# A new order from the latent projection to the heads, expert 2's gate and up loaded early, and the last two experts reordered

## The reference

```
layer 0: x += short_conv_mixer(rms_norm(x));  x += hier_moe(rms_norm(x))
layer 1: x += mla_mixer(rms_norm(x));         x += hier_moe(rms_norm(x))

mla_mixer:  lat = h @ w_down                        # 1024 -> 384 (q) + 256 (kv) + 64 (k rope)
            q = rms_norm(lat_q) @ w_q_up            # 8 heads of 128 + 64
            k_nope, v = rms_norm(lat_kv) @ w_kv_up  # 8 heads of 128 + 128
            per head: rms_norm of q and k, rope on the last 64, softmax(q k') v, then @ w_out
hier_moe:   best group of 8, then best 2 of its 8 experts, for each token;
            y = (silu(x @ w_gate[e]) * (x @ w_up[e])) @ w_down[e],  out += gate * y
```

## Time and profile before

| what | value |
|---|---|
| time, median of 3 runs | 2654.95 us (2654.09 to 2657.17) |
| the profiled execution's own time | 2654.59 us |
| its span, first to last instruction | 2652.9 us |
| PE busy in the span | 2321.1 us (87%) |
| DVE, ACT, POOL busy | 810.5, 627.6, 718.7 us |
| mean granted PE clock | 0.943 of full |
| DMA moved | 693 MB, 261 GB/s over the span |

### The profile page before, as it was taken

The page is one execution under the profiler, slowest core; times in us unless marked ns, Lnnn a source line. Parts: engine busy times, 40 slices in busy tenths (PEclk is TensorE's granted clock), DMA queues, the critical chain, the costliest instruction groups (busy, mean ns, idle before and its releaser), DMA issues. The chain is left out here.

```text
span 2652.9 us, 36216 instructions
## 1 busy us (share of the span) xinstructions
PE 2321.1 (87%) x12364; PEld 1461.0 (55%) x12366; DVE 810.5 (31%) x2114; ACT 627.6 (24%) x1352; POOL 718.7 (27%) x1092
## 2 busy tenths in 40 slices
PE   8999995988888888879799999999588888888886
PEld 6888782433333333349699899878233333333332
DVE  4322443100000000035788888644400000000000
ACT  4000221111111111124366666642011111111111
POOL 3222111222221222213555555211122222222221
PEclk9999997999999999989899999999699999999998
DMA  5111219999999999981000000112999999999997
GB/s 134 48 48 32 80 40 390 422 424 423 424 423 424 424 424 423 424 321 64 10 10 10 18 10 1 64 48 94 375 416 415 413 414 411 417 415 415 412 416 277
DMA packets 138694, 693.02 MB, mean 261 GB/s; under 512 B 38150, under 2 KB 67846, under 8 KB 89456
## 3 DMA queue, kind: packets, MB, share of 16 engines
q1 hardware_dynamic: 114032, 658.26, 60.3%
q0 software_dynamic: 24576, 33.65, 4.4%
HBM read 679.20 MB, written 46.14 MB: 273 GB/s over the span
## 5 line engine op out<-in xcount | busy, mean ns | idle before, releaser
L1460 PE MATMUL ps<-gate_up,arena 128*64 128x384 f32 x2048 | 380.3, 528 | 88.2 <-issue 88.2
L1460 PE MATMUL ps<-arena 128*64 128x384 f32 x2048 | 385.6, 535 | 80.1 <-DMA arena<-in_exp_w_up 78.0
L1360 DVE TENSOR_TENSOR arena<-ps,xw 128x512 f32<-128x512 f32 x128 | 88.5, 691 | 933.3 <-PE ps L1450 933.3
L1460 PEld LDWEIGHTS ps<-gate_up,arena 128*64 128x64 f32 x2048 | 175.0, 148 | 261.8 <-issue 200.6
L1460 PEld LDWEIGHTS ps<-arena 128*64 128x64 f32 x2048 | 156.4, 149 | 278.2 <-issue 230.2
L957 PE MATMUL ps<-hT_split,w_split 128*128 128x512 f32 x1152 | 264.5, 391 | 6.8 <-DVE hT_split L851 6.8
L1229 ACT ACTIVATE arena<-ps 128x384 f32<-128x384 f32 x128 | 62.8, 490 | 866.0 <-PE ps L1460 866.0
L957 PEld LDWEIGHTS ps<-hT_split,w_split 128*128 128x128 f32 x1152 | 216.7, 189 | 52.3 <-DVE hT_split L851 7.4
L1479 PE MATMUL ps<-arena 128*64 128x512 f32 x960 | 223.6, 601 | 0.0
L1369 DVE TENSOR_TENSOR arena<-arena,ps 128x192 f32<-128x192 f32 x128 | 45.3, 354 | 409.7 <-ACT arena L1235 409.7
L1173 POOL DMA_INDIRECT arena<-h_rows,col_idx x128 | 136.0, 1062 | 114.6 <-POOL col_idx L1170 106.0
(11 more groups left out here) (252 smaller groups left out, 3473.9 us busy)
## 6 DMA issues: line engine op xcount, KB each, us to landing
arena<-in_exp_w_down SPq DMA_DIRECT2D x80, 1536.0 KB, 28.7
arena<-in_exp_w_gate SPq DMA_DIRECT2D x64, 1536.0 KB, 31.7
arena<-in_exp_w_up SPq DMA_DIRECT2D x64, 1536.0 KB, 35.6
gate_up<-in_exp_w_gate SPq DMA_DIRECT2D x64, 1536.0 KB, 32.4
gate_up<-in_exp_w_up SPq DMA_DIRECT2D x64, 1536.0 KB, 36.1
down<-in_exp_w_down SPq DMA_DIRECT2D x32, 1536.0 KB, 28.7
x<-in_exp_w_down SPq DMA_DIRECT2D x16, 1536.0 KB, 30.0
arena<-in_conv_w_in SPq DMA_DIRECT2D x24, 512.0 KB, 3.8
```

The source lines that it names most:

```text
L1360: dve.tensor_tensor(xT[:, slot, :, :, :].rearrange("p j h m -> p (j h) m"), c.ps[:, slot, :].rearrange("p (a m) -> p a m", m=RANKS), bc(c. ...
L1460: last_ = pe.matmul(c.ps[row:row + RANKS, 2 + slot, 0:FF], xT[:, slot, j, half, :], w_gate_up[w_slot][:, i, (4 * half + j) * FF:(4 * half ...
```

## The change

- Attention, first part: POOL's `head_tile` and the steps around it run one tile closer to the latents; PE does `up(t-2)` before `latents(t, 1)` and turns early tiles 0 and 1 inside the last latent iteration; the tables are made from t = 0 and used at t = 2. ACT makes the high parts of the eight early tiles (`high_early`, three instructions) in place of DVE, which keeps three of its five. ACT also makes the sum of squares of the rope part of the keys, which DVE made with two instructions. ACT's order becomes `square_lat`, `scale_lat`, the split of the next tile, then `squares(t-2)`.
- `sp_store_rows`: gate and up of expert 2 are issued after the store of tile 5, behind a wait for `y_low_ready`.
- `find_ranks`: two instructions of half the size, and `index_products` waits for each half.
- Last layer only: PE does `down(62)` before `gate_and_up(63)`, and ACT follows.

```diff
@@ sp_store_rows
+            if t == NT - 3:
+                sp.wait_ge(self.y_low_ready, NT - 1)
+                self.experts.load_gate_up(sp, 2, 2)
...
-        self.experts.load_gate_up(sp, 2, 2)
@@ act, experts
-                expert(g0, NE - 1, 1)
+                if last:
+                    copy_y(g0 + NE - 2, NE - 2, 0)
+                    copy_gate_up(g0 + NE - 1, 1)
+                    make_silu(g0 + NE - 1, 1)
+                else:
+                    expert(g0, NE - 1, 1)
@@ find_ranks
-                dve.tensor_tensor(onehot, bc(rank_all, 2, P), ...).then_inc(onehot_ready, 1)
+                for k in range(2):
+                    dve.tensor_tensor(onehot[:, k * NT:(k + 1) * NT, :], bc(rank[:, k, :], 2, P),
...
@@ pe, experts
+                if last:
+                    down(g0 + NE - 2, 0, DOWN_SLOTS - 2)
+                    gate_and_up(g0 + NE - 1, 1, GU_SLOTS - 1)
@@ attention, pool
-                if t >= 2:
-                    head_tile(t - 2)
-            for p in range(NT - 2, TILES):
+                if t >= 1:
+                    head_tile(t - 1)
+            for p in range(NT - 1, TILES):
@@ attention, act
+            def high_early(p):
+                cols = slice(p * P, (p + 1) * P)
+                turned = c.ps[:, EARLY_QK_BANKS[p % 2], :].rearrange("p (j m) -> p j m", m=P)
+                act.wait_ge(qk_turned, p + 1)
+                act.activation(q_split[:, HIGH, :, cols], turned[:, 0:2, :], ACT.Copy).then_inc(qk_high_ready, 1)
+                for j in range(2):
+                    last = act.activation(k_split[:, 0, j, cols], turned[:, 2 + j, :], ACT.Copy,
+                                          scale=qk_gain[:, 2 + j:3 + j])
+                last.then_inc(qk_high_ready, 1)
...
+            for t in range(NT):
                 if t >= 1:
+                    square_lat(t - 1)
+                    scale_lat(t - 1)
                 if t + 1 < NT:
                     split_x(t + 1)
                     square_x(t + 1)
+                if t >= 2:
+                    squares(t - 2)
...
+            square_lat(NT - 1)
+            act.wait_ge(gain_joined, 1)
+            high_early(0)
+            scale_lat(NT - 1)
+            squares(NT - 2)
+            high_early(1)
+            high_early(2)
+            squares(NT - 1)
+            for p in range(3, NT):
+                high_early(p)
+            squares(NT)
@@ attention, dve, after the loop
+            rope_of_keys(NT - 2, NT - 1)
             split_early(0)
+            find_var(NT - 2)
             finish_lat(NT - 1, 0)
+            finish_lat(NT - 1, 1)
             split_early(1)
             rope_of_keys(NT - 1, NT)
             split_early(2)
+            rotate(NT - 2)
             find_var(NT - 1)
             split_early(3)
+            split_early(4)
+            rotate(NT - 1)
+            for p in range(5, NT):
+                split_early(p)
             find_var(NT)
@@ attention, pe
+                else:
+                    turn_early(0)
+                    turn_early(1)
+                if t >= 2:
+                    up(t - 2)
                 latents(t, 1)
...
             turn_latents(NT - 2, 1)
+            up(NT - 2)
             turn_latents(NT - 1, 0)
             turn_early(2)
             turn_latents(NT - 1, 1)
             up(NT - 1)
+            for p in range(3, 6):
+                turn_early(p)
             up(NT)
```

More of the change, by code:

```diff
@@ L1423, in index_products @@
             def index_products(r):
-                pe.wait_ge(onehot_ready, r + 1)
                 for n in range(2 * NT):
+                    if n % NT == 0:
+                        pe.wait_ge(onehot_ready, 2 * r + n // NT + 1)
                     for part in range(2):
@@ L1505, in _ @@
                     expert(g0 + e, e)
-                gate_and_up(g0 + NE - 1, 1, GU_SLOTS - 1)
-                down(g0 + NE - 2, 0, DOWN_SLOTS - 2)
+                if last:
+                    down(g0 + NE - 2, 0, DOWN_SLOTS - 2)
+                    gate_and_up(g0 + NE - 1, 1, GU_SLOTS - 1)
+                else:
+                    gate_and_up(g0 + NE - 1, 1, GU_SLOTS - 1)
+                    down(g0 + NE - 2, 0, DOWN_SLOTS - 2)
                 turn_h(g0 + NE - 1, 1)
@@ L1657, in attention_phase @@
     X_BANKS = (4, 7)
-    TRIG_AT = 2
+    TRIG_AT = 1
     LAT_BANK, EARLY_BANK = 5, 6
@@ L1773, in finish_lat, with scale_lat @@
                                accum_out=lat_sumsq[:, t, 1:2]).then_inc(lat_squares, 1)
+            def scale_lat(t):
+                a, b = 2 * (t % 2), 2 * (t % 2) + 1
                 act.wait_ge(lat_rstd_ready, t + 1)
@@ L1778, in finish_lat @@
                                scale=lat_rstd[:, t, 1:2]).then_inc(lat_scaled, 1)
+                act.activation(c.ps[:, b, KVL + ROPE:KVL + 2 * ROPE], c.ps[:, b, KVL:KVL + ROPE], ACT.Square,
+                               scale=lat_rstd[:, t, 2:3], accum_out=k_rope_sumsq[:, t, 1:2])
                 act.activation(k_raw[:, t, :], c.ps[:, b, KVL:KVL + ROPE], ACT.Copy,
@@ L1794, in squares @@
                 act.activation(raw_place(p), bank[:, 0:QD + NOPE + VD], ACT.Copy).then_inc(raw_copied, 1)
-            for t in range(NT + 1):
-                if t >= 1:
-                    finish_lat(t - 1)
-                if t >= 3:
-                    squares(t - 3)
-                if t == 0:
-                    split_x(0)
-                    square_x(0)
+            def high_early(p):
[7 more added lines that the diff above has]
+                last.then_inc(qk_high_ready, 1)
+            split_x(0)
+            square_x(0)
+            for t in range(NT):
+                if t >= 1:
+                    square_lat(t - 1)
+                    scale_lat(t - 1)
                 if t + 1 < NT:
@@ L1836, in copy_out @@
                                ACT.Copy).then_inc(pair_copied, 1)
-            for p in range(NT - 2, AHEAD_UP):
-                squares(p)
             for s in range(TILES):
@@ L1990, in _ @@
                     tables(k_tmp, k_tmp2, 1)
+                    dve.tensor_tensor(qk_gain[:, 2:3], qk_gain[:, 2:3], qk_gain[:, 0:1], ALU.mult).then_inc(gain_joined, 1)
                     trig.sync()
-                    rope_of_keys(0, 2)
-                if t >= 4:
+                if t >= 2:
                     rope_of_keys(t - 2, t - 1)
+                    find_var(t - 2)
                 if t >= 3:
-                    find_var(t - 3)
-                if t >= 4:
-                    rotate(t - 4)
+                    rotate(t - 3)
             def split_qk(p, bank):
@@ L2140, in turn_qk, with turn_early @@
                 last.then_inc(qk_turned, 1)
+            def turn_early(p):
+                if p == 0:
+                    pe.wait_ge(x_low_ready, 2 * NT)
+                wait(pe, qkT_ready, p - 1)
+                turn_qk(p, EARLY_QK_BANKS[p % 2])
             turn_x(0)
```

48 lines of the change are left out of this document (17 added, 31 removed).

## The result

| | before | changed |
|---|---|---|
| time, median (range), 4 runs each | 2656.06 us (2654.09 to 2658.78) | 2634.64 us (2633.18 to 2638.21) |
| ratio, 95% interval | | 0.9923 (0.9911 to 0.9935), which is 20.5 us |
| span of the profiled execution | 2652.9 us | 2633.4 us |
| mean granted PE clock | 0.943 | 0.948 |

To see where the 19.5 us of the spans came from, I took the same landmark in both traces, and the shift of each. A shift that grows from one line to the next is time gained in between.

What follows compares the result with a forecast made beforehand. Weight transfers bound two stretches, whose starts hang on chains of waits; PE bounds the latents, hand-overs the seam. 11.5 + 0 + 1.7 + 1.6 + 0 + 1.0 = 15.8 us off 2654.6 gives 2638.8 us, range 2633 to 2647.

Steps and rivals of the forecast that it cites:

- The seam: Attention, last latent product to score 0's second half, 34.2 us before; forecast gain 11.5 us, ends 8 and 15.5.
- The walk: Step-by-step timing of the seam in the new order; gains of 10.1, 11.9 or 14.9 us by PE's clock.
- its first delay: In the seam: POOL begins the root for the last latents only at 1272.82, behind a head tile begun at 1269.03.
- up to 7.6 us if ACT's cover were gone: In the seam: the time returning to the chain if ACT's idle time didn't hide the high parts moved there.
- The latent loop: Attention's loop over latents before the seam: 0 forecast, with 2 us lost and 1 won as ends.
- Rival A: Ring of waits over POOL sets the latent loop, 11.9 to 12.3 us an iteration, costing 5 to 7 us; chance 0.12.
- B: Seam gives nothing or time grows: ring over POOL above 14 us an iteration, ending at 2659 at 15; chance 0.06.
- rival D: Head loop starts less far ahead and PE's stalls in first scores take back the seam's gain; 2650.3 us, chance 0.07.
- The one-hot: Routing before each layer's first down: making it in halves gains 1.7 us in layer 0 and 1.6 in layer 1.
- The early load: Expert 2's gate and up issued earlier: 0 us forecast, ends 0 and 3.4 us per layer.
- Rival C: The early load counts in full, 7.5 us per layer, ending at 2624 us; chance 0.05.
- The tail: End of the last layer, `down(62)` ahead of `gate_and_up(63)`: 1.0 us gain taken, 1.2 worked out, 0.3 if scatter 61 is late.

Runs made afterwards that it cites:

- attention alone: The kernel before with only the attention part of the change; median 2645.18 us, ratio 0.9958.
- busy both: Changed kernel plus unused transposes on PE, 80 during each layer's first gather wait and others at the ends of layers; 2632.42 us, ratio 0.9912.
- experiment 7: Changed kernel with POOL's head tiles one iteration later, as before; 2637.90 us, ratio 0.9935, seam 23.07 us.
- experiment 3: Changed kernel with each one-hot made by one instruction again; 2641.10 us, ratio 0.9941.
- experiment 5: Changed kernel with the number of rounds a constant 1 and DVE's counting instructions left out; 2633.70 us, ratio 0.9915.
- experiment 2: Changed kernel with expert 2's gate and up loaded where they were before; 2636.09 us, ratio 0.9924.
- experiment 10: Changed kernel plus unused identity transposes where PE waits at the ends of layers; 2634.43 us, ratio 0.9920, tail 25.62 us.
- experiment 6: Changed kernel with the early tiles' high parts made by DVE again instead of ACT; 2637.66 us, ratio 0.9931, seam 22.77 us.

## Why the prediction was right, and which terms were not

**The seam: 11.5 forecast, 15.8 measured, 15.5 with the loop.** The recorded sign, 20 to 24 us for the seam, was missed: it took 18.5. The walk had three outcomes, 14.9, 11.9 and 10.1 us of gain, by how many `up` run at low clock; I took one slow out of two. In the changed kernel none was slow, in attention alone one (the last), in busy both two, with seams of 18.50, 20.12 and 21.70 us: 1.6 us for each. From the end of the last latent product on, the walk had 17.0, 20.0 and 21.8 us, and the runs 18.4, 20.0 and 21.6. The branch that came true was 1.4 us short: the walk had `up(7)` 6.1 us after the last product, and it came after 7.3, with waits of 0.96 and 0.61 us for DVE to evacuate the last latents. In the other two branches the same shortage is there and hidden, because a slow `up(7)` was priced at 3.0 us, about twice what a slow `up` costs in the runs; that they agree is luck. What failed was the choice of the branch, 1.6 us, and the place of the last product (below), 1.9. As two `up` were slow in before as well, the seams of equal clock are 34.32 and 21.70 us: 12.6 us belong to the order and the move to ACT as such, and about 3.2 to the clock, which stayed full in nine of the eleven kernels with the whole new order. A slip in the working: 1288.1 and the three terms behind it make 1292.4, not 1292.1, and the gain 9.8.

Of its first delay the runs say otherwise: POOL's order was not what put the root early (experiment 7 has the root as early and loses 4.6 us all the same); it puts the head tiles early. The bound "up to 7.6 us if ACT's cover were gone" was measured as 4.3. The chain it stood for is partly parallel.

**The latent loop: 0 forecast, with the last product's end at 1270.3.** (Its own terms, 1268.10 and twice 0.43 and 1.7, make 1270.7.) The product came at 1266.3, which is 0.3 us late against layer 0's shift and not 2.2 later. The two early turns and `up(5)` went into the loop at almost no cost, so 1.9 us were gained here that the sum did not have; that they filled waits of the old loop is my reading of the windows and was not tested. Rival A, the ring over POOL, does not show: PE is busy for 61.99 of 62 us. B has the same condition and falls with it.

**The head loop.** Forecast unchanged, it loses 0.8 us (433.5 to 433.7 us in all kernels with the new order, 432.9 before), 0.5 of it in a new wait for POOL's rows at 1288.55. This is rival D's mechanism, which D priced at all of the seam's 11.5 us. The barrier ahead of layer 1 lost 0.6; over the kernels it varies between 12.0 and 14.0 us with no relation to an edit, and I leave its cause open.

**The one-hot: 1.7 and 1.6 us forecast.** Step to `down(0)` less the first expert: 1.3 and 1.6 us by experiment 3, or 1.4 and 1.8 as means over the kernels with either form. The total was right and its split wrong. The first boundary, counted at 0.8 in each layer, is worth 0 and 0.2, since DVE also waits for its own count of rounds, which ends as late (experiment 5). I had gone by PE's end alone. In before it ended 0.04 us ahead of DVE's step, so nothing looked idle there; that DVE wrote its count and then stood still for 1.16 us up to that same step was the second chain, and I had not priced it. POOL's copy gave its 1.0 us, which is the rule of the shared port again: with the one-hot's boundary half way it waits half as long. The Trainium skill (SBUF — State Buffer, Who interferes with whom) has the loser wait out the whole instruction, and 1.02 against 2.08 us in the pair of kernels that differ in that alone agrees. In layer 1 the second one-hot gave 1.2 instead of 0.85: `turn_h(0)` comes 5.14 us after the first expert's end, 6.31 before. Behind it `gate_and_up(1)` takes 5.68 to 5.74 us in the three profiles with the whole one-hot and 5.38 in all with halves, another 0.3 us of clock that the shorter wait may have saved.

**The early load: 0 forecast, 0 measured** (experiment 2). The deeper dip is there: in layer 0 the DMA share is 0.10 and 0.53 over 440 to 444 us and then again 0.18 and 0.61 over 452 to 456, where the kernel without the early load has only the second dip, 0.42 over 454 to 456. The queue ran dry earlier and waited for `down(0)` all the same. Rival C falls.

**The first experts: no term, 1.9 us.** `gate_and_up(0)` took 0.53 and 1.35 us less than in before, which the sum had as unchanged. No run shows that an edit brings it: over all profiles it lies between 5.38 and 8.31 us. In layer 1 it is 8.19 to 8.31 in the three kernels with the whole one-hot and 6.77 to 8.18 in those with halves and no transposes ahead of it, so whether the one-hot has a part in it stays open. From POOL's copy (without its own length) to the gathered rows' transposes it was shorter as well, by 0.8 us in each layer, which the pair of experiment 3 doesn't repeat (there it is 0.2 us shorter with the halves in layer 0 and 0.2 longer in layer 1).

**The tail: 1.0 forecast, -0.4 in the profiled run, +1.2 in its repetition.** The working, 1.2 us, was right with `down(63)` at full clock. That this product can run at low clock (1.6 us more) was not in it, and which of the two comes is chance as far as two profiles of one kernel show.

In sum: 15.8 forecast, 19.5 measured between the spans. The seam with its loop gave 4.0 more, the first experts 1.9, the rest of the way to `down(0)` 1.3 (1.9 and 2.6 us against 3.3 forecast), DVE's boundary in layer 1 0.2. Taken off are 0.8 in the head loop, 0.6 at the barrier, 0.5 in the two stretches of weights, 0.3 ahead of layer 0's step and 1.4 in the tail. So the mechanism and the order of the terms were right, and the sum was low by 3.7 us because larger misses of both signs partly cancel. The seam with its loop is the largest of them: 1.9 us for the place of the last product, 1.6 for the branch of the clock, 0.4 that I had taken off for what I missed. The full-clock end of the walk, 14.9 us, stood in the prediction. The 1.9 us of the first experts are luck as far as the runs show.

## What to carry to other kernels

When a chain passes tiles between engines, price it once with PE at full clock and once at half, and keep both ends: here 1.6 us hang on each `up`. When a step has two things to wait for, making one of them faster brings only what the other leaves; walk back along both before you count on it, because the trace names one releaser and the two may end together, as PE's products and DVE's own count did here. Effects of 1 to 2 us are to be read from landmarks at the place of the edit, not from the total, in which PE's clock at other places moves as much.

## What was not expected of the hardware

In the stretches of weights, where DMA is the bound, PE comes to wait up to 3.1 us ahead of about every second expert, from `gate_and_up(11)` on in layer 0 and `gate_and_up(22)` in layer 1 of the changed kernel, and that expert's gate and up takes 7.07 us instead of 5.38. The Trainium skill (TensorE: Matmul & The Clock Gate, HAM oscillation — how this bites in real kernels) tells of waits for DMA after which the next tile starts at the lower clock; the trace agrees, and ten idle transposes in that wait made it 5.38 (experiment 10). Within the stretch the wait for weights seems to absorb it, though no run tested that by itself: from `down(0)` to `gate_and_up(62)` of layer 1 it is 705.0 to 706.0 us in every profile. At its last product it costs 1.7 us (experiments 2 and 3). Which of the two comes last differs between kernels whose code up to there is the same (the changed kernel and experiment 6), so a difference of 1.7 us there is no sign of what an edit did.
